# Down-projection weight tiles with two neighbouring rows per partition, in a mixer and mixture-of-experts kernel on one core

## The reference

```python
def _clamped_swiglu(hgu):
    x_glu = jnp.minimum(hgu[..., ::2], SWIGLU_LIMIT)
    x_lin = jnp.clip(hgu[..., 1::2], -SWIGLU_LIMIT, SWIGLU_LIMIT)
    return x_glu * jax.nn.sigmoid(SWIGLU_ALPHA * x_glu) * (x_lin + 1.0)

def _moe_sequence(h, w_router, b_router, w_gate_up, b_gate_up, w_down, b_down):
    ...
    hgu = lax.ragged_dot(xs, w_gate_up, group_sizes) + b_gate_up[e_sorted]
    act = _clamped_swiglu(hgu)
    out = lax.ragged_dot(act, w_down, group_sizes) + b_down[e_sorted]
    out = out * gates.reshape(-1)[order][:, None]
    return jax.ops.segment_sum(out, tok, num_segments=L)
```

## Time and profile before

| What | Value |
|---|---|
| median of 3 runs | 2003.32 us (2002.39 to 2004.54) |
| profiled execution, its own time | 2003.92 us |
| span in its trace, first to last instruction | 2002.2 us |
| granted TensorE clock, mean | 0.985 of full |
| PE, PEld, DVE, ACT, POOL busy | 97%, 77%, 85%, 68%, 20% |
| moved over the span | 533.04 MB, mean 266 GB/s |
| the loop of the experts | from some 755 us to 1980 us of the span |

### The profile page before, as it was taken

One profiled execution on the slowest core, in us unless ns is written; L12 is line 12 of the kernel. 1 busy time (PEld: TensorE's weight loads), 2 busy tenths in 40 slices (PEclk: granted clock), 3 DMA queues, 4 the chain that ended last, 5 costly groups with the idle time before them and its releaser, 6 DMA issues.

```text
span 2002.2 us, 29677 instructions
## 1 busy us (share of the span) xinstructions
PE 1938.2 (97%) x8812; PEld 1540.7 (77%) x8812; DVE 1706.8 (85%) x1759; ACT 1370.1 (68%) x1742; POOL 393.5 (20%) x339
## 2 busy tenths in 40 slices
PE   5999999998989999999999999999999999999998
PEld 2657767786668877888888888888888888888886
DVE  6899977349865479999999999999999999999998
ACT  4456854224345517888888888888888888888885
POOL 6671000000000118211111111111111121111121
PEclk8999999999999989999999999999999999999999
DMA  8232235332010348999999999999999999999995
GB/s 318 76 110 80 84 105 179 117 100 80 22 43 22 78 157 307 384 383 361 378 374 364 380 358 382 380 365 386 358 375 378 361 378 363 367 380 359 383 367 206
DMA packets 152207, 533.04 MB, mean 266 GB/s; under 512 B 14479, under 2 KB 19759, under 8 KB 149408
## 3 DMA queue, kind: packets, MB, share of 16 engines
q1 hardware_dynamic: 136112, 492.45, 65.8%
q0 software_dynamic: 16048, 39.99, 7.7%
HBM read 517.75 MB, written 24.26 MB: 271 GB/s over the span
## 4 chain that ended last, share of the span: by engine, by line
PE 84%; DVE 9%; ACT 3%; issue 1%; DMA 1%; SPq 0%; DVEq 0%; ACTq 0%
PE ps L979 50%; PE ps L1121 4%; PE ps L1169 4%; PE ps L917 3%; PE ps L1112 3%; PE ps L1150 2%; PE ps L1126 2%; PE ps L1345 2%; PE ps L1217 2%; PE ps L885 2%; PE ps L1004 2%; PE ps L856 1%; ACT arena L1801 1%; ACT arena L1799 1%; DVE arena L2556 1%
## 5 line engine op out<-in xcount | busy, mean ns | idle before, releaser
L979 PE MATMUL ps<-split,xTs 128*128 128x512 f32 x3264 | 771.1, 392 | 0.7 <-ACT split L1793 0.5
L979 PEld LDWEIGHTS ps<-split,xTs 128*128 128x128 f32 x3264 | 611.1, 188 | 130.8 <-ACT split L1793 1.2
L2537 DVE TENSOR_TENSOR split<-arena,split 128x2048 fp32r<-128x2048 f32 x204 | 466.9, 2289 | 42.2 <-ACT split L1793 42.2
L2537 DVE TENSOR_TENSOR split<-ring,split 128x2048 fp32r<-128x2048 f32 x204 | 469.2, 2319 | 20.1 <-ACT split L1793 20.1
L1793 ACT ACTIVATE split<-arena 128x1024 fp32r<-128x1024 f32 x408 | 410.0, 1054 | 97.4 <-PE ps L979 94.5
L1793 ACT ACTIVATE split<-ring 128x1024 fp32r<-128x1024 f32 x408 | 410.5, 1055 | 92.6 <-PE ps L979 56.3
L979 PE MATMUL ps<-split,aTs 128*128 128x512 f32 x1632 | 385.3, 391 | 0.1
L979 PEld LDWEIGHTS ps<-split,aTs 128*128 128x128 f32 x1632 | 303.8, 188 | 62.6 <-DVE split L2537 0.6
L1955 DVE TENSOR_TENSOR split<-ring,split 128x2048 fp32r<-128x2048 f32 (+1 forms) x32 | 72.9, 2277 | 68.6 <-ACT split L1456 68.6
L775 POOL DMA_INDIRECT y_rows<-arena,slots x33 | 69.5, 2105 | 269.4 <-issue 250.5
L786 POOL DMA_DIRECT2D slots<-slot_rows x66 | 54.9, 832 | 327.0 <-issue 321.3
(11 more groups left out here) (435 smaller groups left out, 2537.4 us busy)
## 6 DMA issues: line engine op xcount, KB each, us to landing
ring<-in_w_gate_up SPq DMA_DIRECT2D x170, 1024.0 KB
arena<-in_w_gate_up SPq DMA_DIRECT2D x102, 1024.0 KB
arena<-in_w_down SPq DMA_DIRECT2D x102, 1024.0 KB
ring<-in_w_down SPq DMA_DIRECT2D x34, 1024.0 KB
ring<-in_w_in SPq DMA_DIRECT2D x23, 1024.0 KB
ring<-in_w_out SPq DMA_DIRECT2D x8, 1024.0 KB
ring<-in_mod_w SPq DMA_DIRECT2D x10, 512.0 KB, 9.2
ring<-in_mod_w SPq DMA_DIRECT2D x4, 1024.0 KB
```

What stands on the lines that cost most here:

```text
L979: m = mm(ps[:, banks + q, :], lhs[:, x_, k, :], w[:, q * 512:(q + 1) * 512], start=start, stop=stop)
L2537: V.tensor_tensor(split[:, 1, s_, :].rearrange("p a b -> p (a b)"), chunk_pair(p), split[:, 0, s_, :].rearrange("p a b -> p (a b)"), ALU.s ...
```

## The change

The tiles of w_down are loaded so that partition p gets rows 2p and 2p + 1 of the 256. These are neighbours in memory, so the partition's share is one piece of 8 KB in place of two of 4 KB. Chunk 0 of a tile now holds the even rows, chunk 1 the odd rows. The blocks of `actv` that are turned must then hold the even and the odd columns of each 256, so a new `turn_pairs` takes every second column, and it replaces `turn` at the two places where `actv` is turned. The gate-up tiles, whose partition shares are two half rows of 4 KB, 128 rows of 8 KB apart, keep their layout, and so do the turns of `xe`.

```diff
@@ -596,9 +596,11 @@
                 if j < 8:
                     half, g = j // 4, j % 4
                     src = a["w_gate_up_2"][bass.ds(e, 1), g * 256:(g + 1) * 256, half * D:(half + 1) * D]
+                    sp.dma_start(x.rearrange("p (k n) -> p k n", k=2), src.rearrange("o (k p) n -> p (o k) n", p=P)).then_inc(tile_ready[j % SLOTS], 16)
                 else:
+
                     src = a["w_down_2"][bass.ds(e, 1), (j - 8) * 256:(j - 7) * 256, :]
-                sp.dma_start(x.rearrange("p (k n) -> p k n", k=2), src.rearrange("o (k p) n -> p (o k) n", p=P)).then_inc(tile_ready[j % SLOTS], 16)
+                    sp.dma_start(x, src.rearrange("o (p k) n -> p (o k n)", k=2)).then_inc(tile_ready[j % SLOTS], 16)
@@ -917,6 +919,13 @@
+            def turn_pairs(x, bank):
+
+                x = x.rearrange("p (j n k) -> p j k n", j=2, k=2)
+                for k in range(4):
+                    i = nc.tensor.transpose(ps[:, bank, k * P:(k + 1) * P], x[:, k // 2, k % 2, :], IDENT)
+                return i
@@ -1005,7 +1014,7 @@
-                                turn(actv[:, 0:512], 6).then_inc(sig("at_ps"), 1)
+                                turn_pairs(actv[:, 0:512], 6).then_inc(sig("at_ps"), 1)
@@ -1014,7 +1023,7 @@
-                            turn(actv[:, 512:1024], 6).then_inc(sig("at_ps"), 1)
+                            turn_pairs(actv[:, 512:1024], 6).then_inc(sig("at_ps"), 1)
```

## The result

The changed kernel takes 2008.05 us (median of 15 runs, 2005.28 to 2010.86) against 2002.90 us for the kernel before (15 runs): ratio 1.0023, 95% interval 1.0015 to 1.0031. That is slower by 0.23%, 4.6 us by the ratio. The interval excludes no change; it doesn't exclude a size just under the 0.2% that I had set as the limit. My range held the time, but I had forecast no change, at 2003.1 us. The profiled execution took 2008.05 us, its span is 2006.4 us.

A forecast was written before the change was run, and what follows sets the result against it. The prediction took PE to bound the loop, with loads hidden. From 2003.92 us profiled, -0.5 us for loads and +0.3 us for turns gave 2003.7 us; against the median, 2003.32 - 0.2 = 2003.1 us. Range 2001 to 2009 us.

The forecast's parts named there:

- What bounds the kernel: In the loop from 1000 to 1300 us, PE sets the pace at 35.98 us an item; no DMA wait.
- The loads: The w_down loads: 8 KB pieces gain nothing in the steady loop, where PE's work covers all transfers; -0.5 us at the start.
- My saving of 0.24 us a tile: DMA engine time of a w_down tile: 2.89 us in 8 KB pieces against 3.13 us in 4 KB pieces.
- My -0.5 us for the first item: First item, where the pipeline of tiles fills: shorter waits for w_down gain between 0 and 0.9 us, taken as -0.5 us.
- The turns: The 272 transposes of `actv` reading every second float: bounded by 0 to 38 us, taken as +0.3 us from DVE's row.
- Rival B: Transposes of `actv`: weight load longer by over 15 ns; 2007.6 us at 17 ns, 2041 us at 140 ns; chance 0.15.
- The rule on lines: Transposes' reads of SBUF: two hits on each 16-byte line hide its latency, so a step of 8 bytes costs zero.
- Rival C: POOL's queue: 8 KB packets delay the `slots` load for the scatter past L1780's need, some 36 us, 2039 us; chance 0.03.
- Rival D: Matmuls of L979: transfers touch PE's pace, one ns off each gives 4.9 us, 1998.2 us; chance 0.05.
- E: The w_down loads: pieces are cut into 4 KB again, only +0.3 us stays, 2003.6 us; chance 0.03.

## Why the prediction was wrong, step by step

**What bounds the kernel: right.** PE's chain, with the 0.3 us at the end of the activation in it, set the item before, after and in each kernel with the old order.

**The loads: right in the loop, small at the start.** 17408 packets fewer, no gain; loads alone 0.9998. My saving of 0.24 us a tile was too high: I had set the cheapest of three 8 KB tiles against one 4 KB tile. The other two 8 KB tiles (from 187.8 to 193 us and from 200.7 to 206 us) took 57.9% of 5.2 us and 62.1% of 5.3 us, which is 3.01 and 3.29 us, and a second 4 KB tile (from 262.5 to 268 us) 56.6% of 5.5 us, 3.11 us. In the loop, from 850 to 1950 us, q1 took 92.3 to 92.5% in the six profiles with 4 KB loads and 91.6 to 91.9% in the five with 8 KB; over the 120 tiles of w_down in that stretch this makes some 0.06 us a tile, an estimate from these shares. My -0.5 us for the first item can't be told from nothing: its wait moved to other tiles and to the gather, and 0.5 us is within the interval.

**The turns: this is the step that failed.** I had bounded the cost by two rows, DVE's 1% (0.3 us) and ACT's 15% (4.5 us), and took DVE's as the nearest in kind. The turns alone measured +4.2 us. The choice rested on how the pairs of DVE rows and ACT rows compare with each other, and neither says anything of TensorE's weight load. DVE's own price for a step was then measured at 4 ns of 692, so the row was true of DVE, and of DVE only. ACT's 15% came near the sum by chance. It was scaled on the 110 ns of a transpose, and the cost has another form: 65 ns on every load, of which some 10 ns reach the pace, 0.03 us for the block of 4, and one load per item lies open behind PE's wait, which brings the other block to 0.08 us. Both parts could be read in the rows before. A load of 140 ns at a pace of 110 ns is partly covered already, so a longer load isn't paid ns for ns; and the block of 12 took 1.53 us where 12 x 0.110 makes 1.32, so 0.2 us of it lay open at its start.

**Rival B**, the step is paid, was this case, and I gave it 0.15. Its price was not right either. It set a ns of the weight load equal to a ns of PE's time; by that the 65 ns would be 65 x 272 = 17.7 us, far outside the range, and 4.2 us were measured. That 0.12 us over eight transposes is 15 ns, its limit, is luck. Its sign, the 4 transposes at 0.5 us or more and eight times that growth in the item, came only for the block behind the wait: the other took 0.47 us. So the range held the time by luck too, since a load that grew by 65 ns, where the range had room for 20, met a cover that hid most of it. With a bound of 0 to 38 us, the two nearer rows on either side of the limit and nothing that excluded the upper one, an even split was due.

**The rule on lines.** I weighed the Trainium skill's "Advanced Engine Details and Errata", section "Memory Cachelines", for a cost of zero at two hits on a line of 16 bytes. For the weight load of fp32 blocks the runs contradict it: two hits on a line cost 65 ns on a load of 140, and one hit (the step of four) costs no more. For DVE's reads of SBUF the trace agrees, with 696 against 692 ns.

**Rival C** is real in a small size, and I had misread its row. POOL issues two loads of `slots` in an item: one for the next gather (at 1195.05) and one for the scatter (at 1206.87). The 10.9 us of the earlier trace rows belong to the first; for the second, the one that L1780 needs, the trace of the kernel before records no landing. Where it is recorded, from 850 to 1950 us, its median was 5.1 us beside 4 KB pieces (one profile) and 5.3 to 5.5 us beside 8 KB pieces (four profiles), and its longest 5.9 us, against 20.7 us of room. The gather's load is recorded everywhere: a median of 10.0 to 10.1 us in the six profiles with 4 KB pieces, 10.3 to 10.5 us in the five with 8 KB. So POOL's loads do land later beside the longer packets, by some 0.3 us and not by the 10.9 us that I had allowed at the extreme. At the start of the loop the delay is larger. From POOL's load of `slot_first` to its first load for the scatter inside the loop it took 42.5 to 44.8 us with 4 KB loads and 45.5 to 48.9 us with 8 KB loads. There L1789 waited for `slots` once, in three of the five kernels with 8 KB loads (0.3, 1.8 and 1.2 us; 0.3 in the changed kernel) and in none of the six others. It doesn't show in the time of the loads alone. **Rival D** has no sign: L988 takes 391 ns as L979 did, from 1000 to 1300 us. **E** is excluded by the packets.

## What to carry to other kernels

When an edit changes an access pattern on the engine that bounds the kernel, the price must come from that engine and that operand: a row of another engine is a hint and neither a bound nor an estimate, and when rows on both sides of the limit are all there is, "no change" isn't the likeliest case. Ask also what covers the instruction that grows: in a row of like ones most of it can be hidden, and the first one behind a wait is not. Multiply first: 15 ns in an instruction that stands eight times in the bounding chain of 34 items is 0.2% of this kernel. And when a wait ends in a row of like instructions, put first those that don't need what is waited for; here it gave back more than the change had cost, until the next engine's chain set the pace.

## What the runs showed of the hardware

- A weight load of a 128 x 128 fp32 block took 140 ns with neighbours, 208 ns with a step of 8 bytes and 209 ns with a step of 16 bytes (medians).
- In a row of such transposes the pace went from 109 to 118 ns, so most of the longer load runs beside the matmul ahead of it; as the first one after idle time it lies open (a block of 4 took 0.74 us there, 0.48 us behind others).
- DVE's pass over 512 floats with a step of 8 bytes on both inputs took 696 ns against 692 ns (means).
- 8 KB pieces went as single packets, and a tile in them saved some 0.06 us of DMA time (the estimate above), which nothing in this loop could use. A load of 1 KB by POOL beside them landed after a median of 10.3 to 10.5 us, against 10.0 to 10.1 us beside 4 KB pieces.
